# Streaming both parts of the activations past one load of each high weight block in the down projections of a 32-bit transformer kernel

## The reference

```python
def conv_ffn(x, w_gate, w_val, conv_w, conv_b, w_down):
    h = causal_dwconv(x @ w_gate, conv_w) + conv_b
    return (jax.nn.silu(h) * (x @ w_val)) @ w_down
...
        x = layer_norm(ALPHA * x + mixers[layer](x), *ln1[layer])
        x = layer_norm(ALPHA * x + conv_ffn(x, *ffns[layer]), *ln2[layer])
```

## Time and profile before

| | before |
|---|---|
| median of three runs | 3455.18 us |
| lowest to highest | 3450.88 to 3457.72 us |
| the profiled execution, first to last instruction (span) | 3452.7 us |
| median of the runs less that span | 2.5 us |
| TensorE busy | 97% of the span |
| VectorE, ScalarE busy | 65%, 47% |
| TensorE's granted clock, mean of the span | 0.989 of full speed |

### The profile page before, as it was taken

The page is one execution under the profiler, slowest core; times in us unless marked ns, Lnnn a source line. Parts: engine busy times, 40 slices in busy tenths (PEclk is TensorE's granted clock), DMA queues, the critical chain, the costliest instruction groups (busy, mean ns, idle before and its releaser), DMA issues.

```text
span 3452.7 us, 68659 instructions
## 1 busy us (share of the span) xinstructions
PE 3364.0 (97%) x30038; PEld 3308.8 (96%) x30038; DVE 2253.6 (65%) x3653; ACT 1615.7 (47%) x2337; POOL 58.8 (2%) x78
## 2 busy tenths in 40 slices
PE   8999999999999899999999999999999999999997
PEld 8999999999998888999999999998999999999997
DVE  6666555557677787796666655687656966666455
ACT  5444444444455534364444444564443644444443
POOL 1000000000000000000000000001000000000000
PEclk9999999999999999999999999999999999999998
DMA  6555555555564322356555566543444565555663
GB/s 238 174 175 176 184 177 173 182 176 178 175 198 147 98 87 93 105 180 195 192 195 193 191 193 190 188 154 108 153 135 135 169 201 193 194 195 190 188 202 125
DMA packets 162492, 586.36 MB, mean 170 GB/s; under 512 B 18128, under 2 KB 18128, under 8 KB 161936
## 3 DMA queue, kind: packets, MB, share of 16 engines
q1 hardware_dynamic: 160560, 574.01, 50.9%
q0 software_dynamic: 1632, 7.96, 0.7%
HBM read 579.80 MB, written 2.10 MB: 169 GB/s over the span
## 4 chain that ended last, share of the span: by engine, by line
PE 57%; DVE 6%; ACT 1%; issue 1%; POOL 0%; ACTq 0%; DVEq 0%; POOLq 0%
PE bank L2142 17%; PE bank L2144 17%; PE bank L2143 17%; DVE pairs L2935 1%; PE bank L2346 1%; PE bank L2359 1%; DVE xs L3051 1%; DVE xs L3049 1%; PE bank L2157 0%; PE bank L2158 0%; PE bank L2159 0%; DVE xr L2939 0%; DVE right L3399 0%; ACT pairs L2612 0%; ACT xs L2663 0%
## 5 line engine op out<-in xcount | busy, mean ns | idle before, releaser
L2142 PE MATMUL bank<-xr,pairs 128*128 128x256 f32 (+1 forms) x5888 | 1661.4, 282 | 33.2 <-DVE pairs L2935 27.6
L2144 PE MATMUL bank<-xr,pairs 128*128 128x256 f32 (+1 forms) x5888 | 1638.6, 278 | 0.0
L2143 PE MATMUL bank<-xr,pairs 128*128 128x256 f32 (+1 forms) x5888 | 1638.5, 278 | 0.0
L2612 ACT ACTIVATE pairs<-raw 128x1024 fp32r<-128x1024 f32 x1106 | 1142.8, 1042 | 950.5 <-PE bank L2144 750.6
L2935 DVE TENSOR_TENSOR pairs<-raw,pairs 128x1024 fp32r<-128x1024 f32 x1106 | 1308.9, 1202 | 348.2 <-ACT pairs L2612 342.1
L2142 PEld LDWEIGHTS bank<-xr,pairs 128*128 128x128 f32 x5888 | 1114.0, 189 | 45.8 <-DVE pairs L2935 30.6
L2143 PEld LDWEIGHTS bank<-xr,pairs 128*128 128x128 f32 x5888 | 1112.7, 189 | 1.4
L2144 PEld LDWEIGHTS bank<-xr,pairs 128*128 128x128 f32 x5888 | 1112.3, 189 | 0.0
L2142 PE MATMUL bank<-parts,pairs 128*128 128x256 f32 x1792 | 496.5, 277 | 0.4 <-DVE parts L2939 0.4
L2143 PE MATMUL bank<-parts,pairs 128*128 128x256 f32 x1792 | 495.0, 276 | 0.0
L2144 PE MATMUL bank<-parts,pairs 128*128 128x256 f32 x1792 | 495.0, 276 | 0.0
(11 more groups left out here) (602 smaller groups left out, 3047.2 us busy)
## 6 DMA issues: line engine op xcount, KB each, us to landing
raw<-in_w_in SPq DMA_DIRECT2D x176, 512.0 KB, 4.8
raw<-in_gate SPq DMA_DIRECT2D x176, 512.0 KB, 5.6
raw<-in_val SPq DMA_DIRECT2D x176, 512.0 KB, 4.2
raw<-in_down SPq DMA_DIRECT2D x160, 512.0 KB, 4.4
raw<-in_l_w_in SPq DMA_DIRECT2D x144, 512.0 KB, 3.9
raw<-in_w_out SPq DMA_DIRECT2D x64, 512.0 KB, 4.7
raw<-in_l_w_out SPq DMA_DIRECT2D x64, 512.0 KB, 3.9
raw<-in_v_in SPq DMA_DIRECT2D x48, 512.0 KB, 4.7
```

The lines of the kernel that those rows point to most:

```text
L2142: mm(o, wh[:, q, :], rh[:, k, :], start=begin and q == 0, stop=False)
L2143: mm(o, wh[:, q, :], rl[:, k, :], start=False, stop=False)
L2144: last = mm(o, wl[:, q, :], rh[:, k, :], start=False, stop=end and q == c - 1)
L2612: e.activation(pair_of(n)[0], v3(raw_of(n), widths[n] // slices[n]), ACT.Copy).then_inc(*hi_made(n))
```

## The change

In the down projections, for all output tiles but the last two (t = 0 to 13), a high weight block is one instruction: it streams 512 columns, the 256 of the high activations and then the 256 of the low ones, through an operand with a jump in it (`joined`). The high product goes into the first half of a bank, the high-by-low product into the second half. The low weight block streams the high activations as before, into the second half. So a tile fills a bank of its own, and VectorE adds both halves to `x`: with one scalar_tensor_tensor (alpha times x plus the first half) and one tensor_tensor (plus the second half), each of 256 columns. Tiles 14 and 15 and the first block's output projections go the way they went.

```diff
+    def joined(high, low):
+
+        return bass.AP(high.tensor, high.offset, [high.ap[0], (low.offset - high.offset, 2), high.ap[-1]])
+
...
+    def col_tile_parted(keys, rhs, ready, bk):
+
+        k = 0
+        for key in keys:
+            n = load(*key)
+            c = widths[n] // 128
+            do("col_parted", n, bk, rhs, k, key is keys[0], key is keys[-1], [ready_at(ready, k + q) for q in range(c)])
+            pump()
             k += c
         return (used, n)
...
+        def add_parted(t, made):
+            do("x_add_parted", sid, t, alpha, made, xt[t])
+            u = (vec, "x_add", sid, t)
+            for bk, _ in made:
+                banks.put(bk, u)
+            side.append(norm.step(t, u))
+
         for t in range(6 if first else 0, KT, 2):
+            if not first and t < KT - 2:
+                made = []
+                for j in range(2):
+                    bk = mbank()
+                    made.append((bk, col_tile_parted(parts(t + j), y, ready, bk)))
+                add_parted(t, made)
+                continue
             bk = banks.get()
...
+        def col_parted(n, bk, rhs, k0, begin, end, ready):
+            (wh, wl), (rh, rl), c, o2 = pair_of(n), rhs, widths[n] // 128, v3(bk.view, 2)
+            w.wait_ge(*lo_made[n])
+            if begin:
+                w.on(bk.after)
+            for q in range(c):
+                k = k0 + q
+                w.on(ready[q])
+                mm(o2, wh[:, q, :], joined(rh[:, k, :], rl[:, k, :]), start=begin and q == 0, stop=False)
+                last = mm(o2[:, 1, :], wl[:, q, :], rh[:, k, :], start=False, stop=end and q == c - 1)
+            last.then_inc(*used(n))
...
+        def x_add_parted(sid, t, alpha, made, xt):
+            w.on(xt)
+            for j, (bk, m) in enumerate(made):
+                w.on([m])
+                e.scalar_tensor_tensor(out=x[:, t + j, :], in0=x[:, t + j, :], scalar=alpha, in1=bk.view[:, 0:T], op0=MUL,
+                                       op1=ADD).then_inc(*vec("x_add_high", sid, t + j))
+                w.wait_ge(*vec["x_add_high", sid, t + j])
+                last = e.tensor_tensor(x[:, t + j, :], x[:, t + j, :], bk.view[:, T:2 * T], ADD)
+            last.then_inc(*vec("x_add", sid, t))
```

More of the change, by code:

```diff
@@ L576, in col_tile @@
                 pump()
+            k += c
+        return (used, n)
+    def col_tile_parted(keys, rhs, ready, bk):
[5 more added lines that the diff above has]
+            pump()
             k += c
@@ L2581, in ret_pv @@
             mm(ps[:, 128:T], s["v"][:, 1, hh, :], s["A"][:, T:T + 128], start=False, stop=True).then_inc(*pe("ret_pv", j.pr, hh))
-        steps = dict(col_settled=col_settled, norm_cols=norm_cols, col=col, row=row, rms_sq=rms_sq, ln_first=ln_first, norm_sums=norm_sums, scores=scores,
+        steps = dict(col_settled=col_settled, norm_cols=norm_cols, col=col, col_parted=col_parted, row=row, rms_sq=rms_sq, ln_first=ln_first, norm_sums=norm_sums, scores=scores,
                      p_turn=p_turn, pv=pv, rope_mm=rope_mm, kpe_turn=kpe_turn, ukv_k=ukv_k, ukv_v=ukv_v, uq=uq, head_sum=head_sum,
@@ L3563, in vector_program @@
                      norm_acc=norm_acc, norm_var=norm_var, norm_R=norm_R, norm_ln=norm_ln, norm_rms=norm_rms, norm_cols=norm_cols, gains=gains, raw_lo=raw_lo,
-                     lead_fix=lead_fix, lead_scale=lead_scale, x_add=x_add,
+                     lead_fix=lead_fix, lead_scale=lead_scale, x_add=x_add, x_add_parted=x_add_parted,
                      q_scale=q_scale, k_scale=k_scale, k_copy=k_copy, gate_evict=gate_evict, rope_mm=rope_mm, rope_fin=rope_fin, rope_halves=rope_halves,
```

## The result

| | before | changed |
|---|---|---|
| median of four runs | 3454.97 us | 3475.74 us |
| lowest to highest | 3450.88 to 3457.72 us | 3471.6 to 3478.33 us |
| span of the profiled execution | 3452.7 us | 3476.1 us |

The ratio is 1.0059, with a 95% interval of 1.0046 to 1.0071: the changed kernel is 16 to 25 us slower. The forecast was 13 us faster, 3442.0 us. What came is near rival D (16 us slower), to which the prediction gave 0.05.

The account below looks back on a forecast made before the run. TensorE alone was taken to bound the down projections, the weight load setting its step. 1232 blocks x 10.7 ns took 13.2 us off the 3452.7 us span; 3439.5 plus 2.5 gave a median of 3442.0 us, range 3434.5 to 3453.

Parts of the forecast that it names:

- rival D: Down projections: long stream costs two slow steps, next one slow too; 353.1 ns a block, 16 us slower, 3471; chance 0.05.
- at 113.3 ns the weight load sets the step, or the load and the stream together: Down projections: a 256-column stream could be had every 108.6 ns, a load every 111, so the load sets the step.
- Its nearest row is the plain 32-bit matmul with the same array time: New 512-column matmul priced at 216.0 ns from plain 32-bit 256-column matmuls with one 128 x 128 load each.
- The 16 rows: Trace rows taken as 16 plain 32-bit matmuls of 256 columns, (3.62 - 0.38) / 15 = 216.0 ns each.
- Long matmul: Down projections: 512-column matmul with the low block's load hidden under it, 216.0 ns, bounded by 213.3 and 235.4.
- Short matmul: Down projections: 256-column matmul with the next high block's load over it, 113.3 ns; 108.6 if hidden, 117.7 at slower rhythm.
- The block: Down projections: 216.0 + 113.3 = 329.3 ns in place of 340.0, 10.7 ns less in each of 1232 blocks.
- A: Down projections: the load hides altogether, 324.6 ns a block, 19.0 us gained, 3436.2; chance 0.07.
- C: Down projections: step belongs to the columns, removed load was hidden; gain nothing to 3.3 us; chance 0.13 together with E.
- B: Down projections: slower rhythm takes part of the gain, leaving 7.8 us (3447.4) or 2.3 us (3452.8); chance 0.15.
- 216.0 ns is well under two such steps: Argument against the step belonging to columns: 216.0 ns for the plain 32-bit matmul, two of today's steps being 226.7 ns.
- E: Down projections: the load is repeated inside the long instruction, so the same outcome as C; chance 0.13 together with C.

Follow-up runs that it names:

- e10_narrow: Kernel before, with weight blocks of output tiles 0 to 13 of the down projections loaded only 32 columns wide after each tile's first matmul; 3454.19 us in one run.
- e7_bench: Kernel before plus a second set of short matmul series behind its last norm sum; 512 columns over 32-column weights stepped 231 ns, 256 columns 113.3 ns.
- e3_contig: Changed kernel with the long matmul streaming 512 neighbouring columns, two high tiles, in place of high then low activations; 3474.56 us.
- e2_three: Changed kernel with its 512-column matmul cut into two of 256, banks and both VectorE adds kept; 3458.97 us in one run.

## Why the prediction was wrong

**The step that failed** is "at 113.3 ns the weight load sets the step, or the load and the stream together", and with it "Its nearest row is the plain 32-bit matmul with the same array time". The first took two numbers that lie close together, 111 ns between loads and 113.3 between matmuls, for cause and effect. e10_narrow and e7_bench cut the load to a quarter of its columns and 113.3 stayed. The second took a row for the stream that streams at half the pace: at 0.84 ns a column nothing comes on top of the columns' own time, nor does it for fp32r at the clock's lower level (213 ns for 256 columns). At 2.4 GHz a moving fp32r operand costs 0.44 to 0.46 ns a column here, and one column a clock would be 0.42. The 16 rows read as 16 matmuls are also 8 matmuls with two rows each. The two errors held each other up, since 216 ns for 512 columns made 113.3 for 256 look like the load.

**The terms.** Long matmul: forecast 216.0, measured 235.0. Its upper bound in the prediction, two slow steps or 235.4 ns, was what came. Short matmul: forecast 113.3, measured 118.3, near the slow step's 117.7. The block: forecast 329.3, measured 353.3, rival D's 353.1. So the sum's 10.7 ns gained in each block were 13.3 ns lost. Not in the prediction at all: tiles 14 and 15 stay in the slow rhythm behind the long matmuls, 1.16 us in each layer. (The range's lower end, A less 1.5 us, is 3434.7 and not 3434.5; nothing hangs on it.)

**The rivals.** C had the right cause (the step belongs to the columns, the removed load was hidden anyway) but priced it at the fast rhythm. D had the right price, and of its mechanism the place of the reads bears on the step while the jump does not: e3_contig took the jump out and nothing changed. B was right that the place of the operands moves the step; with 229 + 117.6 ns at another place the loss is 5.65 us a stage and no gain. Against C stood only "216.0 ns is well under two such steps", the misread row. E fell with the counts of the page.

**The chances** followed from that. Whether 113.3 ns was load or stream was one open question, and the evidence on one side was one row of another data type. The slow rhythm was known to occur with the same lines and buffers in other stages; that a pattern whose time is all in the columns could be held in it for good was given 0.05.

**What held.** VectorE's doubled adds cost nothing: the first tile's went into the wait, and e2_three kept 240.13 us. No wait of TensorE for another engine appears in either down projection of the changed kernel. Banks, transfers and ScalarE cost nothing.

The operand that stands still takes 216 ns for 512 columns, the moving one 226 to 236. The Trainium skill's page TensorE: Matmul & The Clock Gate (section Back-to-back issue gap) has 2.5 ns over the columns' time: that fits the first and not the second.

**Open**: what in the memory makes 256 moving columns take 113.3 or 117.7 ns, and why the long matmul at the kernel's own placement steps 235 ns in every alternation with a short one, when two long ones in a row step 226 and 236. The runs show that neither a full-width load, nor the jump, nor the banks, nor other engines' work (they rest in the series) is needed for it, and that 64 bytes of placement change it.

## What to carry to other kernels

When two engines' parts that overlap have nearly the same period, shrink one of them (a narrower weight block, an operand that stands still) before saying which sets it; equality is no evidence. Read the price of an instruction from a row of the same data type and pace, since a slower stream can hide the very cost that is asked for. And where a stream has two rhythms, a change of the pattern is to be priced at both, for itself and for the code behind it.

## What the runs showed of the hardware that was not expected

- At the clock's upper level a matmul that streams 512 fp32r columns steps 226 to 236 ns by the place of its operands, and 216 ns if it reads one column 512 times. A weight block of 32 columns in place of 128 leaves 256 columns at 113.3 ns and takes 2 ns off the 233 of 512. At the lower level 256 fp32r columns take 213 ns, their own time at 1.2 GHz and nothing more.
- The pattern of three 256-column matmuls has two rhythms, 113.3 and 117.7 ns a matmul, at the same addresses. Each can last for hundreds of microseconds, and a few small or plain matmuls in between turned the slow one into the fast one. They did not do so for the pair of 512 and 256. Two executions of the same instructions can differ in it (574 or 553 matmuls in the same 65 us), which moves the whole by some 3 us.
- A plain 32-bit matmul leaves two rows in the trace, each with a load: 48 rows for 24 calls, 429 ns a row for 512 columns.
- Cutting a block's instructions and loads by a third made TensorE slower here: 353.3 ns a block against 340.0.
